# Dealing the context pieces of an expert pass in another pattern

## The chip, the cores and the metric

One Trainium2 chip, of which the kernel uses one core. The metric is the device time of one launch in microseconds, lower is better, as the median of several runs. TensorE (PE in the profile) multiplies; VectorE (DVE), ScalarE (ACT) and GpSimd (POOL) do the rest; SyncE (SP) issues DMAs only. 16 DMA engines serve the queues of all of them.

## The reference

Two blocks on 256 tokens of width 1024, all in float32. The first block is a mixer and then a mixture of experts; the second is an mLSTM and pooling mixer and then window attention, on the same tokens `x` and on a context of its own (`ctx_2`). The change lies where the experts of the first block are computed:

```python
for gi in range(N_GROUPS):          # 4 groups of 8 experts
    hid = (jax.nn.silu(jnp.einsum('td,edf->tef', t, w_gate[gi]))
           * jnp.einsum('td,edf->tef', t, w_up[gi])
           * combine[:, gi, :, None].astype(t.dtype))
    out = out + jnp.einsum('tef,efd->td', hid, w_down[gi])
```

`combine` is non-zero for two experts of each token, so every expert has a few tokens, and all 32 experts' weights (3 x 2 MB each) must be read. The second block's mixer over its own context depends on nothing of the first block; its pieces can be computed at any time before.

## The kernel before

*The expert stage.* The tokens of an expert are gathered into a lane group of 32 or 64 rows. The 32 experts are computed in 10 passes (`PASSES`): six of four experts each (passes 0 to 5), then four of two (6 to 9), so a pass fills 128 rows. A pass has six steps: gate half 0 and 1, up half 0 and 1 (line 2462), down half 0 and 1 (line 2479). A step uses one half (1 MB) of a weight of each of the pass's experts. In the trace a step of four or of two experts is 32 or 16 matmuls, since one float32 matmul appears as two.

*The weight slots.* The halves go through nine slots of 1 MB (`half_slot`). SyncE issues the loads in the order of use (`sparse_sync`, line 2301) and holds load n back until `step_used` says that the step that used slot n - 9 is over. With four experts a step frees four slots, and five stay for what comes next. Down steps come behind the gather of the next pass (line 2448), a wait for `hid_out`, transposes of the hidden rows (line 2497), and waits for `gath_out` and `phid_t_out`.

*The context pieces.* Between the steps, `fill(body, p, i)` takes `FILL[p][i]` pieces from a generator of the second block's context mixer. TensorE, ScalarE and VectorE each have such a generator (`body_pe`, `body_act`, `body_dve`), with the same number of pieces, and call `fill` at the same nine places of a pass. On TensorE these are: 0 behind gate half 0; 1 behind gate half 1; 2 behind up half 0; 3 behind the gather that follows up half 1; 4 behind the transposes; 5 behind down half 0; 6, 7 and 8 behind down half 1. ScalarE's wait for both gate halves and its silu stand between its fills 0 and 1, VectorE's product of gate and up between 2 and 3.

The pieces in order: four before pass 0; pass 0: four of v rows, the gate columns (line 1487), then the mLSTM of heads 0 and 1 (lines 1504 to 1538), with four "o" pieces of row halves (1476) dealt among them, one behind every four; pass 1: the rest of that, four z pieces (1460), the head transposes (`heads_pe`, line 1547), one q tile piece (1445); pass 2: tiles of q and k, rows of v, the first mLSTM pieces of heads 2 and 3; pass 3: mLSTM pieces; pass 4: the last of them, four z pieces, the head transposes, eight "pu" pieces, an empty one, two pool pieces (1563); pass 5: two pool pieces, eight "pg" pieces (1445), six of the output projection (1575, 1584). A piece of a tile or of rows is 16 matmuls (8 of 512 columns) of 3.5 us; an mLSTM piece is short.

*The context weights* go through four slots of 1 MB of their own (`f_slot`, NF = 4). A tile needs two. ScalarE issues the two loads for the tile after the next when it takes up the last half of a tile (`f_next`, line 1407), and TensorE waits for them in `w_wait`. At the first pair of the first "pg" tile, ScalarE asks for the second "pg" tile's two halves, as the pool weights' slots are free by then.

Two lines say how a pass is dealt and one how it is used:

```python
FILL_FOUR, FILL_TWO = (2, 2, 2, 2, 2, 2, 2, 1, 1), (0, 0, 0, 1, 0, 1, 0, 0, 0)
FILL[0] = (2, 2, 2, 2, 2, 2, 2, 2, 1)     # FILL[4] alike
for _ in range(FILL[p][i]): next(body, None)
```

Of the kernel before, what the change touches and what calls it, by code (L numbers as in the profile page):

```python
# [227 lines left out]
def build(nc, d, out):  # L228
    ctx = ExitStack()
    with ctx:  # L230
# [2071 lines left out]

        step_of = [n for n in range(6 * NPASS) for _ in range(PASSES[n // 6][1])]

        FILL_FOUR, FILL_TWO = (2, 2, 2, 2, 2, 2, 2, 1, 1), (0, 0, 0, 1, 0, 1, 0, 0, 0)
        FILL = [FILL_FOUR if experts == 4 else FILL_TWO for _, experts in PASSES]
        FILL[0] = (2, 2, 2, 2, 2, 2, 2, 2, 1)
        FILL[4] = (2, 2, 2, 2, 2, 2, 2, 2, 1)

        def fill(body, p, i):  # L2310

# [1179 lines left out]
```

How the kernel before makes its waits and increments, by code:

```python
            def link(self, ins):  # L287
                self.n += 1
                ins.then_inc(self.s, 1)
                self.eng.wait_ge(self.s, self.n)
# [6 lines left out]
        def stage_end(eng, who, marked=False):  # L297
            stages[who] += 1
            if not marked:
                stage_mark(eng)
            eng.wait_ge(stage_done, 3 * stages[who])
# [71 lines left out]
        def chunk_wait(pe, c):  # L374
            _, s, turns, _ = chunks[c]
            pe.wait_ge(slot_filled[s], 16 * turns)
# [9 lines left out]
        def load_chunk(sp, c):  # L387
            src, s, _, displaced = chunks[c]
            if displaced is not None:
                sp.wait_ge(*last_use[displaced])
            sp.dma_start(slot_ap(s), src).then_inc(slot_filled[s], 16)
# [7 lines left out]
        def norm_sum_pe(pe, src, n, ks, lo=0, ahead=0):  # L399
            u = norm_use["pe"]
            q = n // 4
            for k in ks:
                pe.wait_ge(sq_ready, DT * (u - (u > WEIGHTED)) + ahead + k + 1)
                for j in range(4):
                    mm = nc.tensor.matmul(bank[NORM_BANK[u]][32 * j:32 * j + 32, 0:q], ones[:, 0:32], src[:, k, lo + j * q:lo + (j + 1) * q],
                                          start=(k == 0), stop=(k == DT - 1), skip_group_check=True)
                if k == DT - 1:
                    mm.then_inc(sumsq_done, 1)
# [1 line left out]
        def norm_spread_pe(pe, n):  # L411
# [2 lines left out]
            norm_use["pe"] += 1  # L414
            q = n // 4
            pe.wait_ge(rinv_done, u + 1)
            for j in range(4):
```

## Time and profile before

| | us |
|---|---|
| median of 3 runs | 1609.78 (1609.74 to 1610.74) |
| the profiled execution | 1611.13 |
| its span, first to last instruction | 1609.3 |
| TensorE busy | 1517.3 (94%) |
| VectorE busy | 488.3 (30%) |
| ScalarE busy | 344.3 (21%) |
| expert stage, about | 470 to 1070 |

Times in the rows are microseconds from the start of the span. A wait is put down to what came last by the profile; a matmul's end is modelled. Of a chain of work, each row is a stretch that the end of the kernel hung on at that time.

### The profile page before, as it was taken

How to read it: one execution, taken by the hardware profiler on the slowest of the kernel's cores; microseconds unless marked ns; L12 is line 12 of the kernel's file. 1: busy time of each engine (PE TensorE's matmuls, PEld its weight loads, DVE VectorE, ACT ScalarE, POOL GpSimd, SP SyncE). 2: the span in 40 equal slices, each digit the busy share in tenths (PEclk: the TensorE clock that was granted, in tenths of full speed). 3: DMA queues.
4: the chain of work that ended last, by engine and by line, in shares of the span. 5: the costliest groups of instructions: out<-in, count | busy, mean ns of one | idle time of the engine just before them, and what ended most of it. 6: DMA issues, size and time to landing. Idle time of an engine off the chain costs nothing.

```text
span 1609.3 us, 22217 instructions
## 1 busy us (share of the span) xinstructions
PE 1517.3 (94%) x9391; PEld 1055.0 (66%) x9391; DVE 488.3 (30%) x1239; ACT 344.3 (21%) x701; POOL 6.6 (0%) x11
## 2 busy tenths in 40 slices
PE   5999999999899889988899999989999999999997
PEld 3655589888784544635366665458676786878766
DVE  2200066443243421222132000027452241022481
ACT  2311151221122211022110000023322232021571
POOL 0000000000000000000000000000000000000000
PEclk8999999999999999999999999999999999999999
DMA  9989722221369999999999999972222423423100
GB/s 372 419 345 371 297 108 79 105 99 69 119 263 408 419 421 399 413 389 378 418 374 412 420 418 396 408 315 93 105 105 105 157 85 125 157 70 152 53 1 27
DMA packets 54161, 397.07 MB, mean 247 GB/s; under 512 B 6343, under 2 KB 13672, under 8 KB 16296
## 3 DMA queue, kind: packets, MB, share of 16 engines
q1 hardware_dynamic: 40384, 341.85, 52.7%
q10 hardware_dynamic: 13096, 51.64, 8.2%
q0 software_dynamic: 576, 2.10, 0.3%
q8 instruction: 76, 1.25, 0.3%
q14 instruction: 29, 0.24, 0.0%
HBM read 389.80 MB, written 5.77 MB: 246 GB/s over the span
## 4 chain that ended last, share of the span: by engine, by line
PE 83%; DMA 9%; ACT 3%; DVE 2%; issue 1%; SPq 1%; ACTq 0%; PEldq 0%; DVEq 0%; PEld 0%
PE bank L697 16%; PE bank L1445 13%; PE bank L1460 8%; PE bank L2462 8%; PE bank L2479 4%; PE bank L1584 4%; PE bank L1575 3%; DMA ring<-in_moe_w_up 3%; PE bank L529 3%; DMA ring<-in_moe_w_gate 2%; PE bank L2448 2%; DMA work<-in_ada_w 2%; PE bank L728 2%; PE bank L1151 2%; PE bank L1165 2%
## 5 line engine op out<-in xcount | busy, mean ns | idle before, releaser
L697 PE MATMUL bank<-H,ring 128*128 128x256 f32 (+1 forms) x960 | 245.3, 412 | 1.0 <-ACTq L295 0.7
L697 PEld LDWEIGHTS bank<-H,ring 128*128 128x128 f32 x960 | 181.3, 191 | 52.7 <-issue 28.8
L2462 PE MATMUL bank<-ring,work 128*32 128x512 f32 (+1 forms) x712 | 148.3, 629 | 23.6 <-DMA ring<-in_moe_w_gate 8.5
L1445 PE MATMUL bank<-H,work 128*128 128x256 f32 x512 | 116.1, 385 | 0.1
L1445 PE MATMUL bank<-H,ring 128*128 128x256 f32 x512 | 115.9, 387 | 0.0
L2462 PE MATMUL bank<-work 128*32 128x512 f32 (+1 forms) x312 | 109.6, 637 | 0.6 <-DMA work<-in_moe_w_up 0.6
L1445 PEld LDWEIGHTS bank<-H,work 128*128 128x128 f32 x512 | 97.3, 193 | 19.0 <-issue 5.9
L1445 PEld LDWEIGHTS bank<-H,ring 128*128 128x128 f32 x512 | 99.2, 195 | 14.0
L2462 PEld LDWEIGHTS bank<-ring,work 128*32 128x32 f32 (+1 forms) x712 | 40.0, 122 | 97.2 <-issue 70.4
L1460 PE MATMUL bank<-ring,H 128*128 128x512 f32 x192 | 83.4, 593 | 0.0
L2479 PE MATMUL bank<-ring,work 128*32 128x512 f32 (+1 forms) x312 | 69.1, 596 | 0.7 <-issue 0.7
L2479 PE MATMUL bank<-work 128*32 128x512 f32 (+1 forms) x200 | 65.3, 596 | 2.9 <-issue 2.2
L1460 PEld LDWEIGHTS bank<-ring,H 128*128 128x128 f32 x192 | 36.3, 190 | 43.8 <-issue 43.5
L1460 PE MATMUL bank<-work,H 128*128 128x512 f32 x128 | 57.3, 598 | 0.0
L529 PEld LDWEIGHTS bank<-work,csil 128*32 128x32 f32 x1536 | 42.5, 114 | 12.9 <-issue 11.0
L529 PE MATMUL bank<-work,csil 128*32 128x128 f32 x1536 | 49.3, 283 | 0.6 <-DMA work<-in_ada_w 0.6
L1460 PEld LDWEIGHTS bank<-work,H 128*128 128x128 f32 x128 | 23.7, 190 | 31.8 <-issue 31.7
L2462 PEld LDWEIGHTS bank<-work 128*32 128x32 f32 (+1 forms) x312 | 26.9, 122 | 23.0 <-issue 22.0
L2448 PEld LDWEIGHTS bank<-work 128*128 128x128 f32 x320 | 36.6, 192 | 7.5 <-issue 7.5
L2448 PE MATMUL bank<-work 128*128 128x128 f32 x320 | 38.3, 277 | 0.0
L549 DVE TENSOR_TENSOR mod<-bank,vecs 128x8 f32<-128x8 f32 x24 | 4.0, 166 | 106.6 <-PE bank L540 106.6
L1538 PE MATMUL bank<-work 128*128 128x257 f32 x96 | 29.4, 413 | 6.2 <-DVEq L1881 4.1
(449 smaller groups left out, 1999.4 us busy)
## 6 DMA issues: line engine op xcount, KB each, us to landing
ring<-in_moe_w_gate SPq DMA_DIRECT2D x46, 1024.0 KB, 12.8
ring<-in_moe_w_up SPq DMA_DIRECT2D x43, 1024.0 KB, 11.5
ring<-in_moe_w_down SPq DMA_DIRECT2D x39, 1024.0 KB, 13.4
work<-in_ab_w_in ACTq DMA_DIRECT2D x28, 1024.0 KB, 9.9
ring<-in_ab_w_in SPq DMA_DIRECT2D x14, 2048.0 KB, 7.5
work<-in_moe_w_down SPq DMA_DIRECT2D x25, 1024.0 KB, 14.6
work<-in_ada_w SPq DMA_DIRECT2D x12, 2048.0 KB, 15.4
ring<-in_w_in SPq DMA_DIRECT2D x12, 2048.0 KB, 9.8
```

The costliest lines, as they stand in the source:

```text
L529: mm = nc.tensor.matmul(bank[5][32 * g:32 * g + 32, 0:P], csil[:, m // 12, k, :], slot_k(mod_chunk[m], k, g * P, (g + 1) * P), start=(k == ...
L697: mm = nc.tensor.matmul(tile_bank(i)[:, 0:n], weight(c, k, j * P, (j + 1) * P), rhs(k), start=(k == 0), stop=(k == kt - 1))
L728: mm = nc.tensor.matmul(bank[i % NB][:], H[:, k, t * P:(t + 1) * P], slot_k(c, k, 0, 512), start=(k == 0), stop=(k == DT - 1))
L1151: mm = nc.tensor.matmul(bank[4 + j % 2][:, half * T:(half + 1) * T], slot_w(c, k, j * P, (j + 1) * P), y[:, k, :], start=(k == 0), stop=(k ...
L1165: mm = nc.tensor.matmul(bank[6 + j % 2][:, 0:T], slot_k(c, k, (j % 4) * P, (j % 4 + 1) * P), mix[:, k, :], start=(k == 0), stop=(k == DT - 1))
L1445: mm = nc.tensor.matmul(b[:, j * T:(j + 1) * T], w_k(m, n, k, at, at + P), H[:, k, m.s], start=(k == 0), stop=(k == DT - 1), skip_group_ch ...
L1460: mm = nc.tensor.matmul(b[:], H[:, k, at:at + P], w_k(m, n, k, 0, 512), start=(k == 0), stop=(k == DT - 1))
L1575: nc.tensor.matmul(b[:, j * T:(j + 1) * T], w_q(m, OUT[r], 8 + k, j * P, (j + 1) * P), m.yp[:, k, :], start=(j + k == 0), stop=False, skip ...
L1584: mm = nc.tensor.matmul(b[:, j * T:(j + 1) * T], w_q(m, OUT[r], k, j * P, (j + 1) * P), m.ym[:, k, :], start=False, stop=(k == 7), skip_gr ...
L2448: mm = nc.tensor.matmul(bank[2 + k // 4][:, (k % 4) * P:(k % 4 + 1) * P], hrows[:, t, k * P:(k + 1) * P], pick[:, t, :], start=(t == 0), s ...
L2462: mm = nc.tensor.matmul(bank[b][rows, :], gath[:, k, rows], half_slot[(load_at[n + half] + e) % NHALF][:, (k % 4) * 512:(k % 4 + 1) * 512] ...
L2479: mm = nc.tensor.matmul(bank[2 + side][rows, :], phid_t[:, f, rows], half_slot[(load_at[n + half] + e) % NHALF][:, at:at + 512], start=(f ...
```

## The change

The tuple of pieces of a four-expert pass, and those of passes 0 and 4, which have one piece more, are replaced. The sums stay 16 and 17. The two-expert passes keep theirs.

```diff
-        FILL_FOUR, FILL_TWO = (2, 2, 2, 2, 2, 2, 2, 1, 1), (0, 0, 0, 1, 0, 1, 0, 0, 0)
+        FILL_FOUR, FILL_TWO = (3, 2, 3, 1, 1, 3, 1, 1, 1), (0, 0, 0, 1, 0, 1, 0, 0, 0)
         FILL = [FILL_FOUR if experts == 4 else FILL_TWO for _, experts in PASSES]
-        FILL[0] = (2, 2, 2, 2, 2, 2, 2, 2, 1)
-        FILL[4] = (2, 2, 2, 2, 2, 2, 2, 2, 1)
+        FILL[0] = (3, 2, 3, 1, 1, 3, 2, 1, 1)
+        FILL[4] = (3, 2, 3, 1, 1, 3, 2, 1, 1)
```

## Rows read from the trace of the kernel before

**Rows 1.** The page: what the DMA engines moved, the span in 40 slices.
```profile
GB/s 372 419 345 371 297 108 79 105 99 69 119 263 408 419 421 399 413 389 378 418 374 412 420 418 396 408 315 93 105 105 105 157 85 125 157 70 152 53 1 27
```

**Rows 2.** The chain of work, passes 0 and 2: start, length, engine and line.
```profile
487.84 3.57 PE bank L2462 x32
...
660.85 3.57 PE bank L2462 x32
664.42 3.77 PE bank L2448 x32
668.19 3.46 PE bank L1445 x16
...
682.38 3.57 PE bank L2479 x32
```

**Rows 3.** TensorE's waits from 470 to 1070: us in total, times, longest.
```profile
PE bank L2462 <- DMA ring<-in_moe_w_gate: 8.5, 2, 6.6
PE bank L2462 <- DMA ring<-in_moe_w_up: 7.5, 3, 3.8
...
PE bank L2462 <- DMA work<-in_moe_w_gate: 4.5, 1, 4.5
PE bank L2462 <- DMA work<-in_moe_w_up: 3.6, 2, 3.0
```

**Rows 4.** Windows: stretch, busy PE, PEld, DVE, ACT, POOL, clock, DMA share, GB/s.
```profile
500.00:510.00 10.00, 10.00 (x48) 3.71 (x44) 0.00 (x0) 1.00 (x2) 0.00 (x0) 1.00 1.02 419
...
620.00:640.00 20.00, 18.40 (x96) 13.14 (x100) 5.28 (x12) 1.20 (x3) 0.00 (x0) 0.83 0.94 377
683.00:687.00 4.00, 4.00 (x31) 1.29 (x24) 0.00 (x0) 0.00 (x0) 0.00 (x0) 1.00 0.47 195
751.00:757.00 6.00, 6.00 (x44) 2.81 (x43) 0.01 (x1) 0.38 (x1) 0.00 (x0) 1.00 0.54 225
829.00:836.00 7.00, 7.00 (x48) 3.71 (x47) 0.00 (x0) 0.59 (x1) 0.00 (x0) 1.00 0.45 147
```

**Rows 5.** The chain of work, loads and the steps behind waits.
```profile
560.56 3.69 PE bank L2462 x32
...
763.03 21.48 DMA ring<-in_moe_w_gate
...
809.35 4.59 PE bank L2462 x32
...
889.16 5.34 PE bank L2462 x32
```

**Rows 6.** TensorE in order of time: two steps, with the idle time before them.
```profile
560.56 0.62 PE L2462 MATMUL bank<-ring,work 128*32 128x512 f32 x1 [1.92 <-DMA ring<-in_moe_w_gate]
...
889.16 0.62 PE L2462 MATMUL bank<-ring,work 128*32 128x512 f32 x1 [3.80 <-DMA ring<-in_moe_w_up]
```

**Rows 7.** In order of time: ScalarE's and TensorE's part in the gate columns, pass 0.
```profile
509.15 0.94 ACTq L1407 DMA_DIRECT2D work<-in_ab_w_in  x2
...
513.20 0.71 PE L1487 MATMUL bank<-ident,work 64*128 64x64 f32 x8 [0.52 <-ACT work L1645]
```

**Rows 8.** In order of time: the first mLSTM product behind its set-up, pass 3.
```profile
745.64 0.67 PE L1527 MATMUL bank<-work 128*128 128x257 f32 x2 [2.06 <-DVE work L1864]
```

**Rows 9.** In order of time: before the head transposes of pass 4.
```profile
807.65 1.70 PE L1547 MATMUL bank<-ident,work 128*128 128x128 f32 x8 [3.75 <-DVE work L1941]
```

**Rows 10.** TensorE in order of time: context pieces of passes 4 and 5.
```profile
849.70 3.62 PE L1445 MATMUL bank<-H,work 128*128 128x256 f32 x16
...
867.51 7.17 PE L1445 MATMUL bank<-H,work 128*128 128x256 f32 x32
...
898.10 7.07 PE L1445 MATMUL bank<-H,work 128*128 128x256 f32 x32
```

**Rows 11.** DMA issues from 853 to 855, then from 874 to 876: median us to landing.
```profile
work<-in_ab_w_in ACTq DMA_DIRECT2D x2, 1024.0 KB, 10.4
...
work<-in_ab_w_in ACTq DMA_DIRECT2D x2, 1024.0 KB, 12.1
```

## The prediction, made before the changed kernel ran

> **What bounds the kernel now.** The page first: in slices 13 to 26 of 40, that is from 483 to 1046 us, the DMA engines move 374 to 421 GB/s, about all that any slice shows [rows 1]. That is the expert stage. TensorE (PE) is nearly always busy there too, so I read the stage as a race between the two. An expert step of a four-expert pass takes TensorE 3.57 us and frees four slots; refilling them moves 4 x 1.049 MB, which at 420 GB/s takes 10.0 us. A full context piece is 16 matmuls in 3.5 us [rows 2]. A pass has 16 pieces, so with full pieces TensorE needs 6 x 3.57 + 3.77 (gather) + 0.44 (transposes) + 16 x 3.5 = 82 us, and the transfers need 60 us for the experts and 20 us for 8 MB of context weights. In passes 2, 4 and 5 nearly all pieces are full and TensorE is the later one; passes 1 and 3 hold mostly short mLSTM pieces, and the transfers are.
>
> The waits of TensorE in the stage say what that costs: 8.5 + 7.5 + 4.5 + 3.6 = 24.1 us for gate and up weights [rows 3]. The windows say what the other side loses [rows 4]. Between two freed steps the queue holds at most 12.5 us of expert loads, and the longest distance between two frees is 21.5 us: up-half 1 ends at 664.42, the down step at 685.95, with gather, four pieces and transposes between [rows 2]. There the queue runs dry: a loss against 420 GB/s of 20 x 43/420 = 2.0 us near 630, 4 x 225/420 = 2.1 at 683, 6 x 195/420 = 2.8 at 751 and 7 x 273/420 = 4.6 at 829 [rows 4]. What is lost is paid later: the load that pass 4's gate half 1 waits for lands only 21.48 us after its issue, at 784.52 [rows 5]. After that of pass 5's up half 1 at 889 [rows 6] no load is late and the stage ends by TensorE alone.
>
> **The change part by part.** Nothing is added or removed: every pass deals as many pieces as before (16, or 17 in passes 0 and 4), each matmul and load is there, and all passes begin at the same piece. The two-expert passes don't change. So all is in who waits.
>
> *The distances.* With full pieces the frees of a pass came after 10.6, 10.6, 10.6, 21.5, 10.6 and 17.6 us; now it is 3, 2, 3, (1+1), 3 and 3 pieces: 14.1, 10.6, 14.1, 14.8, 14.1 and 14.1 us. None is far over the 12.5 us of the queue, and context loads fill the rest. The losses near 630 (2.0), 751 (2.8) and 829 (4.6) should go. The one at 683 I keep: its distance falls to 14.8, but the one ahead of it grows to 14.1, and no context load is asked for between the last k piece, ahead of up half 1, and the last v piece, behind down half 0. A new one comes at the very start: step gate-half 1 of pass 0 ends at 491.41 + 3 x 3.53 + 3.57 = 505.6 us [rows 2], one piece later than before, while the four loads released at 491.4 and what was left of two context loads are through at about 503; before, that stretch was full [rows 4]. Loss 2.6 us.
>
> *Up to the landing of pass 4's gate half 1* (784.52 [rows 5]), which waits for transfers in both kernels, the sum of the losses counts: -2.0 - 2.8 + 2.6 = -2.2 us. Against it, in pass 0, the piece of gate columns now follows its release at once and not after an expert step: ScalarE's release let it start at 513.20, and the last v piece was through by 509.15, so the wait is 4.0 in place of 0.52 us [rows 7]. An mLSTM set-up piece and the first product behind it stand side by side in pass 0 and 2 too; that cost 2.06 us where they do now, in pass 3 [rows 8]. Both frees of pass 0 come some 6 us later by it, still about within the queue. With one piece in place of two behind gather and transposes, the cover of ScalarE's and VectorE's copies is 3.8 + one piece; where the piece is an mLSTM one of under 1 us, some tenths show. For all that I add 1.2 us (bounds 0 and 4). Up to here -1.0 us.
>
> *From there on* the order of the waits changes, in four places:
> 1. Pass 4's head transposes stood right behind the last z piece and waited 3.75 us; the expert step behind them ran 4.59 us in place of 3.57 [rows 5, 9]. Now that step lies between, 3.57 us long, and hides all but 0.2. Gain 3.6 + 1.0 = 4.6 us.
> 2. Pass 5's up half 1 waited 3.80 us for its load and ran 5.34 us in place of 3.57 [rows 5, 6]. With the loss at 829 gone its load lands 4.6 us sooner, while TensorE comes later (3 and 4). Gain 5.6 us.
> 3. The context weights of the first "pg" tile are asked for when the last "pu" tile is through (849.70 + 3.62) and wanted at 867.51: 14.2 us later, with two expert steps and four pool pieces between [rows 10]. Now only one step lies between: 10.6 us. The two loads took 10.4 us in the mean [rows 11], the second some 1.6 more: 12.0. In a full queue two context loads took 12.1 in the mean [rows 11], and as the second is behind by one load at half of 420 GB/s (5.0 us, less 0.4 between the issues), it landed after 14.4. A new wait of 1.4 to 3.8 us; 3.2 taken, since the queue is now full there.
> 4. The second "pg" tile's weights are asked for at the end of the first pair (867.51 + 7.17 = 874.7), wanted at 898.10 [rows 10]. Between them now lie piece, step, piece: 10.6 us. A new wait of 14.4 - 10.6 = 3.8 us, less whatever that step waits for its own load.
> Behind the waits of 3 and 4 the clock can fall, as at 889 (1.77 us) or not, as behind the wait of 1.92 us at 560.56, where the step took 3.69 [rows 5, 6]: 0 to 3.5 us, 1.8 taken. Sum: -4.6 - 5.6 + 3.2 + 3.8 + 1.8 = -1.4 us.
>
> Two rules of the Trainium skill bear on this. In "DMA: Bandwidth & Descriptors", section "Queues, rings and completion order", a DMA engine takes turns between the queues that have work, packet by packet: an expert queue that is never empty halves a context load for its whole length. The trace agrees (12.1 us where the queue was full, 10.4 where it had a gap), and the rule speaks against this change; by it item 3 is 3.8 us and the sum below -1.8; by the gap's row it would be 1.4 and -4.2. "TensorE: Matmul & The Clock Gate", section "HAM oscillation — how this bites in real kernels", has the clock fall on waits for DMA between bursts; the steps at 889 and 809 agree, that at 560 doesn't.
>
> **The sum.** -1.0 - 1.4 = -2.4 us. The profiled execution took 1611.13 us (its span 1609.3 and 1.8 around it) and would take 1608.7. The median of the runs shown is 1.35 us under the profiled one, 1609.78; so 1607.4 us.
>
> **The rivals.** *The context weights aren't late* (20%): if the loads of items 3 and 4 hide under expert steps that wait for their own load, their 8.8 us mostly vanish. Bound: -10.2 + 1.4 + 0.5 = -8.3, and -2.2 before it: down to -10.5; its middle is -7.5, 1602.3 us. For it: in this very pass an expert load is 3.80 us late now [rows 6]. Against: by the change that load lands 4.6 us earlier.
> *The new waits outweigh* (24%), the one on the slower side: TensorE runs dry for context weights twice in pass 5 with nothing to cover it, at full price with the clock: 3.8 + 3.8 + 3.5 = 11.1 against the 10.2 won; and in passes 0 to 3, where the transfers set the pace, the 2.6 us lost at the start are carried on and half of what is to be regained is not (+1 to +4). Together +3.5, 1613.3 us. It decides as soon as the waits of pass 5 with their slow steps pass 10.2 us less what the first part brings.
> *Evener frees bring nothing* (10%): the lost transfer time only moves, as the new gaps of 14.1 us are themselves over 12.5, and items 1 to 4 cancel: 0 +- 1, 1609.8 us.
> The forecast itself has 46%, reaching from -5.5 to +0.7 us.
>
> **How the numbers follow.** A run of this kernel can be told from no change from about 0.2% on, 3.2 us. Faster by more: the first rival's 20% and two fifths of the forecast's 46%: 0.38. Slower by more: over three fourths of the second rival: 0.19. Within: the rest, 0.43. The range leaves out the outer halves of the two far cases: 1601.0 to 1614.0.
>
> **What would show it.** In the changed profile: the windows near 630, 751 and 829 (a few microseconds shifted) at 400 GB/s or more, and a dip near 504. The head transposes of pass 4 without their 3.75 us. A new row in TensorE's waits: line 1445 behind a DMA of in_ab_w_in, twice, 1.4 to 3.8 us each; the waits of line 2462 for gate and up weights down from 24 to some 12 us. The sum is wrong if the frees of pass 0 come so late that passes 1 and 3 wait longer than before, or if the "pg" tiles don't wait.

## The result: slower by 0.36%, and the profile after

The changed kernel takes 1616.4 us, the kernel before 1610.3 us (medians of 8 runs each). The ratio is 1.0036, 95% interval 1.0020 to 1.0053, so some 5.8 us slower. Single runs of one kernel lie up to 10 us to either side of its median, so verdicts below rest on ratios with intervals, and a profile tells where time lies, not how much the change is worth to a microsecond. The profiled execution of the changed kernel took 1621.1 us, with a span of 1619.3.

The chain of work has the last expert step before, and, in the second fence, the first step, pass 4's gate half 1 and the last step after:

```profile
1066.07 3.58 PE bank L2479 x16
```

```profile
487.24 3.57 PE bank L2462 x32
...
791.09 5.02 PE bank L2462 x32
...
1076.17 3.58 PE bank L2479 x16
```

From the first expert step to the last, before took 1066.07 - 487.84 = 578.2 us [rows 2] and after 588.9: all of the 10 us between the two profiles lies in the expert stage. It comes in two portions. Pass 4's gate half 1 starts 303.9 us after the first step in place of 296.7 [rows 2, 5]: 7.1 us, worked out before rounding. The rest of the stage adds 3.6.

The windows next, in the columns of [rows 4]. The first fence has a stretch at the start of the stage and one near its end before, the second the same two after. The third fence is of the changed kernel alone: stretches where the queue runs dry now, and two, at 751 and 829, where it ran dry before.

```profile
480.00:550.00 70.00, 67.53 (x401) 38.07 (x399) 30.15 (x99) 14.23 (x28) 0.00 (x0) 1.00 1.00 413
...
860.00:945.00 85.00, 81.20 (x460) 55.54 (x458) 6.93 (x12) 5.71 (x10) 0.00 (x0) 0.98 1.01 418
```

And the changed kernel:

```profile
480.00:550.00 70.00, 62.91 (x340) 34.39 (x338) 25.90 (x87) 12.67 (x24) 0.00 (x0) 0.90 0.91 361
...
860.00:945.00 85.00, 78.27 (x455) 53.50 (x454) 16.92 (x27) 4.75 (x8) 0.00 (x0) 0.97 0.92 370
```

```profile
504.00:507.00 3.00, 3.00 (x17) 1.06 (x6) 0.00 (x0) 0.60 (x1) 0.00 (x0) 1.00 0.42 101
521.00:524.00 3.00, 3.00 (x25) 1.46 (x18) 0.36 (x1) 0.00 (x0) 0.00 (x0) 1.00 0.42 104
534.00:536.00 2.00, 2.00 (x18) 2.00 (x19) 0.69 (x1) 0.00 (x0) 0.00 (x0) 1.00 0.60 131
545.00:548.00 3.00, 2.77 (x17) 1.66 (x10) 1.16 (x4) 0.00 (x0) 0.00 (x0) 1.00 0.67 186
...
620.00:630.00 10.00, 7.98 (x42) 2.38 (x40) 1.66 (x4) 2.00 (x4) 0.00 (x0) 1.00 0.83 322
640.00:646.00 6.00, 6.00 (x41) 3.76 (x34) 0.00 (x0) 0.00 (x0) 0.00 (x0) 1.00 0.92 294
694.00:700.00 6.00, 6.00 (x30) 2.26 (x23) 0.00 (x0) 0.00 (x0) 0.00 (x0) 1.00 0.60 206
...
751.00:757.00 6.00, 6.00 (x46) 5.69 (x46) 2.32 (x5) 1.77 (x3) 0.00 (x0) 1.00 1.01 418
829.00:836.00 7.00, 7.00 (x48) 3.71 (x47) 0.00 (x0) 0.59 (x1) 0.00 (x0) 1.00 1.02 418
...
879.00:882.00 3.00, 3.00 (x24) 1.70 (x13) 0.00 (x0) 0.60 (x1) 0.00 (x0) 1.00 0.28 52
...
939.00:943.00 4.00, 4.00 (x29) 2.55 (x20) 0.69 (x1) 0.58 (x1) 0.00 (x0) 1.00 0.44 125
```

The losses at 751 and 829 are gone, as forecast. The one at 683 stayed, as forecast; with all else it lies some 10 us later, at 694 to 700: 6 x 214/420 = 3.1 us. The one near 630, which should have gone too, did not: 10 x 98/420 = 2.3 us at 620 to 630 and 6 x 126/420 = 1.8 us at 640 to 646. New are four dry stretches in pass 0 and several in pass 5, of which the fence shows two. Between 480 and 550 alone 70 x (413 - 361)/420 = 8.7 us of transfers are missing.

TensorE's waits in the stage, in the form of [rows 3]:

```profile
PE bank L1527 <- DVE work L1864: 7.3, 3, 3.0
PE bank L1563 <- issue: 7.0, 1, 7.0
PE bank L1445 <- issue: 4.5, 1, 4.5
PE bank L2479 <- DMA work<-in_moe_w_down: 4.3, 1, 4.3
PE bank L1547 <- DVE work L1941: 4.0, 2, 3.8
PE bank L1487 <- ACT work L1645: 4.0, 1, 4.0
...
PE bank L2462 <- DMA ring<-in_moe_w_gate: 3.1, 1, 3.1
...
PE bank L2462 <- DMA work<-in_moe_w_up: 2.8, 2, 1.5
...
PE bank L1563 <- DVE work L2009: 2.3, 1, 2.3
...
PE bank L2462 <- DMA work<-in_moe_w_gate: 0.4, 1, 0.4
```

The waits for gate and up weights fell from 24.1 to 3.1 + 2.8 + 0.4 = 6.3 us, with one of 4.3 us for down weights new, and the head transposes (L1547) wait 4.0 us in place of 7.5. Yet 7.3 + 7.0 + 4.5 + 4.0 + 2.3 = 25.1 us, of L1527, L1563 twice, L1445 and L1487, stand where 2.06 and 0.52 stood [rows 7, 8]. ("issue" means that the profile names nobody who ended the wait; the two cases are worked out below.)

Pass 0 in the chain of work after, the counterpart of [rows 7]:

```profile
504.88 3.65 PE bank L1460 x8
...
512.48 1.11 PE bank L1487 x8
513.59 3.31 PE bank L1493 x16
516.90 5.54 PE bank L2462 x32
522.45 1.07 PE bank L1504 x4
...
527.19 0.72 PE bank L1527 x2
```

The wait before the gate columns (L1487) is 508.5 to 512.48; behind it the granted clock is 0.50 (1.2 of 2.4 GHz) up to 516.9 and 0.64 in the mean from there to 522.4: the columns take 4.42 us in place of 2.45, and up half 0 5.54 in place of 3.57. Up half 0 frees its slots at 522.45, in the kernel before at about 512.7.

Passes 4 and 5 in the chain of work after:

```profile
830.06 24.32 DMA work<-in_pool_inv
854.40 1.31 DVE work L1976
...
890.99 3.65 PE bank L1445 x16
894.64 4.46 issue
899.11 8.83 PE bank L1445 x32
```

The constants that VectorE needs for the pool pieces take 24.32 us to land, up to 854.38. VectorE's first product for TensorE is made from them behind that, and TensorE's wait of 7.03 us ends at 857.99; the pool piece then takes 5.77 us in place of 3.63. In front of the second "pg" tile TensorE waits 4.46 us for its weights: the second of its two loads takes 14.6 us and lands at 899.0, and the tile starts at 899.11. It then runs 8.83 us for what is 7.1.

### The profile page after: what moved, and what is told of

Same layout as the page of the kernel before. It is cut to its first block, busy times and chain, and to the rows that moved or that the text cites. A ratio compares the mean times of both kernels' runs of the same rounds, so it can differ in the third digit from the quotient of the medians.

```text
span 1619.3 us, 22218 instructions
## 1 busy us (share of the span) xinstructions
PE 1523.6 (94%) x9391; PEld 1058.1 (65%) x9391; DVE 488.4 (30%) x1239; ACT 345.7 (21%) x702; POOL 6.6 (0%) x11
## 3 DMA queue, kind: packets, MB, share of 16 engines
HBM read 389.80 MB, written 5.77 MB: 244 GB/s over the span
## 4 chain that ended last, share of the span: by engine, by line
PE 83%; DMA 7%; DVE 3%; ACT 3%; issue 2%; SPq 1%; ACTq 0%; DVEq 0%; PEldq 0%; PEld 0%
PE bank L697 16%; PE bank L1445 13%; PE bank L1460 8%; PE bank L2462 8%; PE bank L2479 4%; PE bank L1584 4%; PE bank L1575 3%; PE bank L529 3%; PE bank L2448 2%; PE bank L728 2%; DMA work<-in_ada_w 2%; PE bank L1151 2%; PE bank L1165 2%; DMA work<-in_moe_w_up 2%; DMA work<-in_pool_inv 2%
## 5 line engine op out<-in xcount | busy, mean ns | idle before, releaser
L1445 PE MATMUL bank<-H,work 128*128 128x256 f32 x512 | 118.0, 389 | 4.6 <-issue 4.5
L1445 PE MATMUL bank<-H,ring 128*128 128x256 f32 x512 | 115.6, 386 | 0.0
L1445 PEld LDWEIGHTS bank<-H,work 128*128 128x128 f32 x512 | 98.3, 195 | 24.3 <-issue 10.7
L1445 PEld LDWEIGHTS bank<-H,ring 128*128 128x128 f32 x512 | 99.1, 195 | 14.0
L2462 PEld LDWEIGHTS bank<-ring,work 128*32 128x32 f32 (+1 forms) x712 | 39.4, 121 | 75.7 <-issue 67.5
L2462 PEld LDWEIGHTS bank<-work 128*32 128x32 f32 (+1 forms) x312 | 26.0, 119 | 24.7 <-issue 22.9
L2479 PEld LDWEIGHTS bank<-ring,work 128*32 128x32 f32 (+1 forms) x312 | 18.7, 121 | 29.4 <-issue 29.4
## 6 DMA issues: line engine op xcount, KB each, us to landing
work<-in_ab_w_in ACTq DMA_DIRECT2D x28, 1024.0 KB, 10.2
work<-in_moe_w_down SPq DMA_DIRECT2D x25, 1024.0 KB, 12.5
```

The costliest lines, as they stand in the source:

```text
L1445: mm = nc.tensor.matmul(b[:, j * T:(j + 1) * T], w_k(m, n, k, at, at + P), H[:, k, m.s], start=(k == 0), stop=(k == DT - 1), skip_group_ch ...
L2462: mm = nc.tensor.matmul(bank[b][rows, :], gath[:, k, rows], half_slot[(load_at[n + half] + e) % NHALF][:, (k % 4) * 512:(k % 4 + 1) * 512] ...
L2479: mm = nc.tensor.matmul(bank[2 + side][rows, :], phid_t[:, f, rows], half_slot[(load_at[n + half] + e) % NHALF][:, at:at + 512], start=(f ...
```

## The experiments

Each ratio is against the kernel before, timed on the same chip in the same rounds. Tuples are those of one pass, the others as said.

**Pass 0, put back.** The changed kernel, pass 0 old.

```diff
-        FILL[0] = (3, 2, 3, 1, 1, 3, 2, 1, 1)
+        FILL[0] = (2, 2, 2, 2, 2, 2, 2, 2, 1)
```

> The changed kernel with pass 0 dealt in the old pattern (2,2,2,2,2,2,2,2,1), all else changed. Theory 1 (the transfers' queue runs dry in pass 0 because TensorE frees slots late there: wait of 3.97 us for the gate columns, 2.16 us for the first mLSTM product, steps at the slow clock behind them; 6.3 us lost between 470 and 550): the stretch 480 to 550 is back at about 413 GB/s, pass 1's gate half 0 begins near 553 and not 562.5, and the kernel is 4 to 8 us faster than the changed one, about 1610. Theory 2 (what counts lies in passes 4 and 5; time lost in pass 0 is made good in pass 2, where TensorE is the later one): within 2 us of the changed kernel, about 1616.

1605.9 us, ratio 0.9976 (0.9958 to 0.9993). The stretch 480 to 550 moved 397 GB/s, and pass 1 began 67.6 us behind the first step in place of 75.3; before it was 65.3. The 2.3 us that are missing aren't the other passes' doing: from the gate columns to the end of the set-up piece TensorE took 7.35 us, most of it at a granted clock of 0.50, in place of 4.87 at 1.00 before. The old pass 0 ran so in two of the six profiles that have it; in the other four pass 1 begins after 65.1 to 65.5 us. Without the new deal of pass 0 the change is a gain: 0.60% of the ratio is pass 0's. Theory 2 falls.

**Pass 0 alone, changed.** The kernel before with `FILL[0] = (3, 2, 3, 1, 1, 3, 2, 1, 1)`.

> The kernel before with pass 0 alone in the new pattern (3,2,3,1,1,3,2,1,1). Theory 1: 470 to 550 loses 6 us of transfers, pass 1 begins 9 to 10 us late, and 4 to 7 us of it are left at the landing of pass 4's gate half 1 and at the end: about 1614 to 1617. Theory 2: lost time is made good in pass 2; within 2 us of the kernel before.

1616.2 us, ratio 1.0032 (1.0013 to 1.0051). The same waits in pass 0 (3.97 us at the gate columns, 2.16 at the first product), 346 GB/s from 480 to 550, pass 1 begins 11.1 us later than before, and the last step of the stage 5.1, counted from the first.

```profile
480.00:550.00 70.00, 63.49 (x339) 34.54 (x338) 25.76 (x85) 12.20 (x23) 0.00 (x0) 0.90 0.87 346
550.00:630.00 80.00, 70.24 (x403) 35.74 (x401) 20.43 (x55) 19.51 (x37) 0.00 (x0) 0.98 1.01 419
```

Pass 0 alone costs 5 us on the old kernel, and 0.60% (10 us) where the other passes are dealt anew. The intervals of the two figures overlap, so whether they differ at all stays open.

**Which piece of pass 0.** The kernel before with one piece moved, in two ways.

```diff
-        FILL[0] = (2, 2, 2, 2, 2, 2, 2, 2, 1)
+        FILL[0] = (2, 3, 1, 2, 2, 2, 2, 2, 1)   # gate columns ahead of up half 0
+        FILL[0] = (3, 1, 2, 2, 2, 2, 2, 2, 1)   # three pieces ahead of gate half 1
```

> The kernel before with one piece of pass 0 moved: (2,3,1,2,2,2,2,2,1), so that the gate columns follow the last v piece at once and not behind up half 0; every other free of a slot stays where it was. Theory G (the wait for ScalarE in front of the gate columns, 3.97 us in the changed kernel, and the slow clock behind it are what empties the queue): up half 0 ends some 7 to 9 us later than before, 2 to 4 us of transfers are lost between 470 and 550, and 3 to 5 us of the 5 us that pass 0 costs appear, about 1613 to 1615. Theory F (the longer first distance, three pieces between the first two frees, is the cause): within 2 us of the kernel before.

1614.9 us, ratio 1.0028 (1.0012 to 1.0044). The gate columns wait 3.97 us, up half 0 ends 9.7 us later than before, counted from the first step, and 480 to 550 moves 383 GB/s: 5.0 us of transfers are lost, more than expected.

> The kernel before with one piece of pass 0 moved the other way: (3,1,2,2,2,2,2,2,1), three pieces between gate half 0 and gate half 1 and one behind it; the gate columns stay behind up half 0. Theory F: gate half 1 frees its slots 3.5 us later, 1.5 to 2.5 us of transfers are lost near 504, and 2 to 3 us are left at the end, about 1612. Theory G: the loss at 504 is there but is made good, within 1.5 us of the kernel before.

1610.4 us, ratio 1.0001 (0.9986 to 1.0015). The one piece that puts the gate columns right behind the last v piece costs as much as the whole new pass 0. The longer first distance loses 3 x 341/420 = 2.4 us of transfers at 504, as worked out, and by the times none of that shows at the end, to within 2.4 us. The profile of this run doesn't say so as clearly: its last expert step comes 3.9 us later than before, counted from the first (7.7 in the run with the gate columns moved). 2.4 us of that were there at the end of pass 0, where this execution had the slow clock behind the gate columns as well. So theory G holds, and the step that it names costs more than the first distance; that F's 2 to 3 us are nought is not shown, as they lie at the edge of the interval.

**The same piece within the changed kernel.** `FILL[0] = (3, 1, 4, 1, 1, 3, 2, 1, 1)`, all else as changed.

> The changed kernel with one piece of pass 0 moved: (3,1,4,1,1,3,2,1,1), so that up half 0 stands between the last v piece and the gate columns again, all else as changed. Theory G (the exposed wait in front of the gate columns is the cause of most of what pass 0 costs): the wait of 3.97 us is down to about 0.5, pass 1 begins 4 to 6 us sooner, and the kernel is 3 to 6 us faster than the changed one, 1610 to 1613. Theory S (the set-up piece, the product behind it and the slow clock are as much of it): less than 2 us faster.

1612.7 us, ratio 1.0008 (0.9986 to 1.0031), some 4.5 us under the changed kernel by the ratios. Its gate columns wait 0.41 us. The intervals of the two kernels overlap, so this run agrees with theory G without settling it; the two single moves above say more. Pass 0 in full back is a further 0.32%, and whether that is the set-up wait (line 1527 behind L1864) wasn't tried.

**Pass 4, put back.**

> The changed kernel with pass 4 dealt in the old pattern (2,2,2,2,2,2,2,2,1). Theory 1 (pass 0 carries the loss): the landing of pass 4's gate half 1 stays some 7 us later than in the kernel before; no more than 3 us faster than the changed kernel. Theory 2 (the pool weights, asked for at the end of the first pu tile while the expert queue was full, took 21.6 and 24.3 us to land in place of 5.5 and 6.3, and that made the wait of 7.0 us at line 1563): the old pattern empties the expert queue there, the pool weights land within 8 us, the wait at 1563 goes, the head transposes wait 3.75 us again, and the kernel is 4 to 7 us faster than the changed one.

1619.5 us, ratio 1.0054 (1.0033 to 1.0075): not faster but, if anything, slower. Theory 1's half is right (pass 4's gate half 1 stays late). The pool weights landed within 5.4 and 6.3 us, as theory 2 said, the wait at 1563 went, and its gain did not come: pass 5 waited 7.1 us for "pg" weights, gate half 1 of pass 4 7.0 us for its load.

**Pool weights in long runs.**

```diff
-    a["ab_pool_w_2"] = i["ab_pool_w_2"][0]
+    a["ab_pool_w_2"] = i["ab_pool_w_2"][0].reshape(len(POOLS), 2, P, MD).transpose(2, 0, 1, 3).reshape(P, 2 * len(POOLS), MD)
```

> The changed kernel with one more change: the pool weights lie in DRAM as TensorE's slot wants them, one run of 8 KB per partition in place of eight runs of 1 KB; same bytes, same issue. Theory A (a queue gets its turns by packet, so 1 KB runs get an eighth of the bytes of the expert queue's 8 KB runs and the load is slow whenever the expert queue is full): the two pool loads land after 10 to 14 us, the wait at line 1563 goes, 6 to 10 us faster than the changed kernel. Theory B (the loads were slow for another reason, as the state of the queue or memory): still over 18 us, and within 2 us of the changed kernel.

1613.8 us, ratio 1.0020 (1.0003 to 1.0038). In landing times theory A is right. DMA issues of the changed kernel, then of this one (us to landing last):

```profile
work<-in_ab_pool_w ACTq DMA_DIRECT2D x1, 1024.0 KB, 21.6
work<-in_pool_inv ACTq DMA_DIRECT2D x1, 512.0 KB, 24.3
```

```profile
work<-in_ab_pool_w ACTq DMA_DIRECT2D x1, 1024.0 KB, 9.1
work<-in_pool_inv ACTq DMA_DIRECT2D x1, 512.0 KB, 12.5
```

In time it isn't: the ratio is 0.16% lower, less than the intervals tell apart. TensorE in order of time shows the wait one tile on, where it was forecast at first:

```profile
847.38 3.63 PE L1563 MATMUL bank<-work 128*128 128x256 f32 x16
854.50 3.73 PE L1563 MATMUL bank<-work 128*128 128x256 f32 x16
861.63 6.38 PE L1445 MATMUL bank<-H,work 128*128 128x256 f32 x16 [3.39 <-issue]
...
890.48 8.83 PE L1445 MATMUL bank<-H,work 128*128 128x256 f32 x32 [4.57 <-issue]
```

**The head transposes alone.** The kernel before with `FILL[4] = (3, 2, 1, 2, 2, 2, 2, 2, 1)`.

> The kernel before with one piece of pass 4 moved: (3,2,1,2,2,2,2,2,1), so that up half 0 stands between the last z piece and the head transposes. No other distance of pass 4 changes by more than one piece. Theory 1 (from pass 4's gate half 1 on, TensorE is the later one, so a wait of TensorE that goes is won): line 1547's wait of 3.75 us in pass 4 goes with the slow step behind it, 3 to 5 us faster than before, about 1605 to 1607. Theory 2 (the expert load of pass 5's up half 1 takes it back, its wait grows from 3.80 to some 7 us): within 1.5 us of the kernel before.

1609.6 us, ratio 1.0000 (0.9984 to 1.0015). Nothing. TensorE's waits from 785 to 860, here and then before:

```profile
PE bank L2464 <- DMA ring<-in_moe_w_up: 7.0, 1, 7.0
PE bank L1547 <- DVE work L1941: 0.2, 1, 0.2
```

```profile
PE bank L2462 <- DMA ring<-in_moe_w_gate: 6.6, 1, 6.6
PE bank L1547 <- DVE work L1941: 3.7, 1, 3.7
```

(Lines behind the pattern are two further down in this kernel.) The wait of 3.75 us is down to 0.2, and up half 1, the step right behind the transposes, waits 7.0 us for its load. In the kernel before it waited not at all: a piece and the transposes' wait had hidden that the load was late. The moved piece itself went ahead of gate half 1, whose wait is 3.2 us here, just ahead of the stretch shown, in place of 6.6. Theory 2 has the time right but not the place, which is pass 4 and not pass 5.

**Pass 5, put back.**

> The changed kernel with pass 5 alone dealt as before. The wait for the second pg tile's weights, 4.46 us and a slow step of 1.7 us behind it, goes. If pass 5 is TensorE's, as its expert loads' lead of 10 to 14 us in the changed kernel says: 4 to 7 us faster than the changed kernel, 1609 to 1612. If another wait takes its place: within 2 us of it.

1608.3 us, ratio 0.9999 (0.9984 to 1.0014): 0.37% under the changed kernel. The wait for the second "pg" tile went, 860 to 945 moved 415 GB/s in place of 370, and the whole slowdown is cancelled by it though pass 0 still has its loss.

**Both put back, with the long runs and without.** Passes 0 and 5 old, 1 to 4 as changed.

> What the runs so far point to: passes 0 and 5 dealt as before, passes 1 to 4 as in the changed kernel, and the pool weights in DRAM as runs of 8 KB. If the losses of the changed kernel are the ones named (pass 0's late frees, the late pool weights in pass 4, the second pg tile's weights in pass 5), none of them is left: the waits at 1563 and at 1445 go, and it is 8 to 12 us faster than the kernel before, 1598 to 1602. If the even deal of passes 1 to 4 brings nothing by itself, it is level with the one with pass 0 old, 1604 to 1608.

1602.8 us, ratio 0.9948 (0.9930 to 0.9966).

> The kernel with passes 0 and 5 dealt as before and passes 1 to 4 as changed, but the pool weights in DRAM as before, in runs of 1 KB. Against the one with runs of 8 KB (1602.8, 0.52% under the kernel before). Theory A (the pool load's small runs cost their wait wherever the expert queue is full): pool loads land after 13 to 24 us, a wait at line 1563 of 2 to 9 us, 1604 to 1608. Theory N (the layout is worth nothing in time): 1602 to 1603.

1598.4 us, ratio 0.9945 (0.9912 to 0.9977). Both beat the kernel before by half a per cent, and by the ratios the changed one by 0.9%. Theory N holds for the layout: here the pool loads took 21.7 and 24.7 us again, the wait at 1563 was 7.4 us, and the time is the same. From pass 4's gate half 1 to the start of pass 6 the two take 152.3 and 153.7 us (before 156.2, changed 159.8): what TensorE doesn't wait for at the pool pieces it waits for at the expert loads.

```profile
480.00:550.00 70.00, 67.57 (x400) 37.70 (x398) 29.97 (x98) 15.23 (x28) 0.00 (x0) 1.00 1.00 412
550.00:630.00 80.00, 71.59 (x404) 36.61 (x403) 17.26 (x45) 17.65 (x33) 0.00 (x0) 0.94 1.01 420
630.00:700.00 70.00, 66.72 (x364) 38.76 (x363) 17.50 (x42) 11.08 (x20) 0.00 (x0) 0.98 0.99 401
700.00:785.00 85.00, 73.97 (x446) 38.65 (x445) 19.48 (x53) 19.41 (x37) 0.00 (x0) 0.98 1.01 420
785.00:860.00 75.00, 64.92 (x382) 42.32 (x384) 24.55 (x39) 5.99 (x10) 0.00 (x0) 0.95 0.99 402
860.00:945.00 85.00, 85.00 (x488) 55.41 (x478) 5.91 (x11) 6.31 (x11) 0.00 (x0) 1.00 1.01 418
```

These are the windows of the kernel with short runs: the transfers hardly pause from 480 to 945.

**Pass 4 alone, with the long runs.** The kernel before, pass 4 as changed.

> The kernel before with pass 4 alone dealt as changed, and the pool weights in DRAM as runs of 8 KB: tells how much of the gain of the mixed kernel is pass 4's and how much that of passes 1 to 3. If the queue's losses at 829 and the head transposes' wait are what is won: 4 to 6 us faster than before, 1604 to 1606. If the even deal of passes 1 to 3 is needed for it (the load of up half 1 lands too late for TensorE to use the room): within 2 us of before.

1601.9 us, ratio 0.9960 (0.9942 to 0.9979). Most of the gain of passes 1 to 4 is pass 4's: 0.40 of 0.52%. What is left for passes 1 to 3 is within the intervals.

**Where the time lies in the profiles.** In microseconds: pass 0; from there to the start of gate half 1 of pass 4; from there to the start of pass 6; and the last expert step against that of the kernel before, counted from the first step. From the start of pass 6 on all kernels take 125.2 or 125.3 us. The last column is what the ratio of the timed runs says.

| | pass 0 | to pass 4 | to pass 6 | last step | timed |
|---|---|---|---|---|---|
| before | 65.3 | 231.5 | 156.2 | 0 | 0 |
| changed | 75.3 | 228.6 | 159.8 | +10.7 | +5.8 |
| before, pass 0 new | 76.4 | 225.5 | 156.2 | +5.1 | +5.2 |
| before, gate columns moved | 71.3 | 231.9 | 157.4 | +7.7 | +4.5 |
| before, longer first distance | 67.7 | 232.7 | 156.5 | +3.9 | +0.2 |
| changed, pass 0 old | 67.6 | 228.0 | 155.1 | -2.3 | -3.9 |
| changed, pass 5 old | 74.9 | 229.6 | 151.5 | +3.0 | -0.2 |
| changed, passes 0 and 5 old, short runs | 65.1 | 225.3 | 153.7 | -8.9 | -8.9 |
| before, pass 4 new, long runs | 65.5 | 230.7 | 152.8 | -4.0 | -6.4 |

The two last columns differ by up to 5 us, as a profile is one execution: a row tells where time is lost, the last column what it costs. Where pass 0 alone is new it takes 11.1 us longer, and 6.0 of them come back up to pass 4. With passes 1 to 3 new the second stretch is 2 to 6 us shorter.

## Why the prediction was wrong, step by step

It said 1607.4 us, slightly faster, in a range of 1601 to 1614; the time is 1616.4 and the sign is the other. What came is most like the second rival, a loss at the start carried on and two waits for context data with slow work behind them, though the first of these stands at the end of pass 4 and not in pass 5; it had 24% and a price of +3.5.

**The distances between frees in passes 1 to 4: right in the main.** The losses near 751 and 829 went and the one at 683 stayed, as said. The one near 630 did not go but grew from 2.0 to some 4 us (620 to 646); with passes 0 and 5 old it went or nearly went, with 420 and 397 GB/s over 620 to 640 in the two kernels, where before moved 377. The waits for gate and up weights fell by 18 us (forecast 12), in part only because TensorE came later. Passes 1 to 4 dealt evenly are worth half a per cent, most of it pass 4's.

**Pass 0 is the step that failed.** The working had the waits right: 4.0 us in front of the gate columns (3.97 measured), 2.06 for the first product (2.16), both frees "some 6 us later", in fact 10.4 and 12.8 (up half 0 and 1, counted from the first step). It then let them pass as "still about within the queue" and gave 1.2 us for it. Two errors. First, the clock: behind the 3.97 us the gate columns and up half 0 took 2.0 us more each, while the sum charged slow steps only in pass 5. No run separates the clock's part from the wait's. Second, the queue's 12.5 us were used as an allowance of each distance. They are a stock, and once it is used up a step brings back only the 10.0 us that it frees. After the first long distance of 14.1 us every further microsecond over the transfers due is lost: the frees at 504.9, 522.5, 534.0 and 545.6 are 17.6, 11.5 and 11.7 us apart; 10.0 us of expert loads, and 5.0 of context loads in the first of them, leave 2.6, 1.5 and 1.7, and the windows at 521, 534 and 545 show 3 x 316/420 = 2.3, 1.4 and 1.7 us. In all, pass 0 costs about 5 us by itself, and about 10 beside the other new passes. The loss of 2.6 us at the first distance was in the sum; the run with that piece alone is level, to within 2.4 us.

**Item 1, the head transposes: the gain was not there to be had.** Its premise, that TensorE is the later one from pass 4's gate half 1 on, was not checked with the steps in between. Alone the move is worth 0.0%, since the load of up half 1 was due only then. The whole of pass 4 dealt anew is worth 0.40%; which of its moves brings that was not tried.

**Item 2: right.** Pass 5's up half 1 no longer waits.

**Item 3: the wait came sooner, at the pool pieces.** The price was worked out for the "pg" weights, 1.4 to 3.8 us. The pool loads issued before them were not looked at; before they had landed within 6.3 us, now the later one took 24.3 in a full queue. TensorE waited 7.03 and 2.27 us at the pool pieces, terms that the sum put at nothing, and with that the "pg" weights were in time. Where the pool weights were made fast, the forecast wait stood there with 3.39 us.

**Item 4: right in place, low in size.** 4.46 us in place of 3.8, and 1.7 us of slow clock. (The prediction counts the slow step at 809 among those behind waits for DMA; it stood behind a wait for VectorE [rows 9].) As put, items 3 and 4 and the clock were 8.8 us against 10.2 us won. Measured by the runs, pass 5 dealt anew costs 0.37%, 6 us.

By the runs, in place of -2.4, some 8.5 us are won by passes 1 to 4, 5 to 10 lost in pass 0 and 6 in pass 5: +2.5 to +7.5, and +5.8 was measured.

The prediction cites a rule of the Trainium skill for item 3 ("DMA: Bandwidth & Descriptors", section "Queues, rings and completion order"): a DMA engine takes turns between the queues that have work, packet by packet. It was applied to the "pg" weights and not to the pool weights, the load that a full expert queue slowed most, with runs of 1 KB (21.6 us, against 9.1 us in runs of 8 KB). The landing of 5.5 us in the kernel before did not show that, as the transfers ran at 147 GB/s there and the expert queue was nearly empty [rows 4].

## What to carry to other kernels

A pool of slots that one engine frees and a queue fills is a stock: add up frees and transfers from the start, and charge every microsecond beyond the stock. Before a piece is moved, look at what it and its successors wait for on the other engines; a wait that an expert step hid is exposed when that step moves, with the slow clock behind it. And treat a wait that goes as won only when the next step's load has landed by then.

## What the runs showed of the hardware that I had not expected

A load of 1 MB in runs of 1 KB landed after 5.5 us while the other queue was empty, and after 21.6 us while it was full; the same bytes in runs of 8 KB took 9.1 us in a full queue. The load behind it, 512 KB, was held up with it: 24.3 against 12.5 us.

The clock can differ between executions of the same work. The gate columns and the pieces up to up half 1 of the old pass 0, behind a wait of 0.40 us, took 4.9 us at a granted clock of 1.00 in two profiles and 7.2 to 7.4 us, most of it at 0.50, in two others.
